# Expert rows spread over their half of the partitions, and every other pair of experts with its halves exchanged

## The chip, the cores and the metric

The kernel runs on one core of one Trainium2 chip, as one program and one launch. The time is that of the device in microseconds (us), as the median over runs. "The profiled execution" is one run recorded by the hardware profiler; positions in it are us from the start of its span. The core has five engines with queues of their own: PE (TensorE, with PEld for its weight loads), DVE (VectorE), ACT (ScalarE), POOL (GpSimd) and SP (SyncE, which here only issues DMAs), and sixteen DMA engines that all of them share. Every DMA raises its semaphore by sixteen, one for each DMA engine, and a wait for it asks for all sixteen.

## What is computed

Two transformer blocks follow one another on 512 tokens of width 1024, in fp32. The first mixes a sliding-window attention, a forgetting attention and a recurrent unit and ends in a dense feed-forward layer. The second mixes an mLSTM and a differential attention and ends in a layer of experts. Only this last layer is touched by the change:

```python
def hierarchical_moe(h, ...):        # h: 512 x 1024
    g_idx = top group of 4           # from h @ w_rg + b_rg
    j_idx = top 2 of the 8 experts of that group      # from h @ w_re + b_re
    combine = one_hot(e_idx) * weights                # 512 x 32, two entries a row
    for e in range(32):
        act = silu(h @ w_gate[e]) * (h @ w_up[e])     # 1024 -> 256
        y = y + combine[:, e:e+1] * (act @ w_down[e]) # 256 -> 1024
```

A token takes two experts, both of one group, so 1024 rows are worked in all, 32 an expert on average. The reference's own router, evaluated on the inputs, gives these counts for experts 0 to 31:

```
39 70 43 25 39 44 50 74   35 40 48 23 34 23 28 19
32 18 11 17 13 16 15 18   16 27 16 44 45 47 14 41
```

Experts 0 to 15 get 650 rows and experts 16 to 31 get 374.

## The kernel before, in words

**Dense part.** Nearly all of the time goes to dense products over 2048-column slabs of weights (`SLABS`). SP loads a slab, ACT rounds it to a high part `WH` (L975), DVE takes the rest `WL` (`feed`, L1505), and PE makes three products of high and low parts (L2354 to L2356). A slab's products begin once its `WL` is there (`lo_ready`, L2362). Their sums lie in four banks of PSUM in turn, and DVE or ACT evicts them (L2045 for the last projection `wo2`). `begin(s)` on DVE puts small work ahead of a slab's split: at the slab `("wo2", 0)` it calls `routing_numbers` (L1936), which makes constant tables, and then `feed`, which splits the slab after it.

**The expert layer.** A *tile* is a pair of experts with 128 rows of tokens: partitions 0 to 63 (half 0) for the one, 64 to 127 (half 1) for the other; `CAP` = 64 rows an expert. Expert x below 16 stands in half 0 and x + 16 in half 1 of the same tile. Tiles 0 to 2 hold experts 0 to 2 with 16 to 18; tile 3 (`OVER`) holds the rows beyond 64 of experts that have more (here 6 rows of expert 1 and 10 of expert 7); tile t from 4 to 16 holds experts t - 1 and t + 15. Further tiles run under a branch that is not taken here.

*Routing on DVE.* `places[:, 0]` is 0 or 64 by expert (its half), `places[:, 1]` its tile. The rank of a token within its expert comes from products with a triangular matrix (`ranks`); `row` is rank plus half (up to L2250). `inrow` (L2252) compares `row` with `iota`, a table of 128 numbers along the free axis that is 0, 1, 2 ... 127, and so says for each token which of the 128 partitions it takes; `here` (L2256) does so for the tile, with the first numbers of `iota`. Two sets of small products turn these into `tok` (the token of each partition and tile, or a number out of bounds for an empty place) and `wtab` (the weight).

*POOL* gathers with an indirect DMA the rows of a tile from `h2_dram` into `Xg` (L911, two buffers), and after the tile adds its rows `Yt` to `out` with an indirect DMA that accumulates (L929). Each takes 128 partitions of 4 KB, and places out of bounds are left out. The order of issue is gather(t + 2), scatter(t). A scatter waits for the one before it to have landed. For tile 3 there are two scatters, one for each half, the second behind the first.

*SP* loads an expert's weights: gate and up, 1 MB each, then down, 1 MB, into one of six slots (`SLOTS`, three tiles). Each is a DMA of 128 partitions with 8 KB in each. Tiles 0 to 2 are loaded early, each half at a place of its own among the slabs. From tile 3 on `load_pair` issues gate and up of both experts, once tile t - 3 has used its slots (`gu_done`), and then both downs, once `y_done` of tile t - 3 is reached (L746, L756).

*PE*, for each tile: `gate_up` (L2902, 32 products with 512 columns), the transposes of the next tile's rows (L2880), two transposes of the activations (L2888), `down` (L2919, 16 products). ACT and DVE do silu, the product, the copies and the weighting between them. `gate_up(t)` waits for its weights with all sixteen of each DMA:

```python
for half in halves(t):
    pe.wait_ge(*when(f"gu_landed{(2 * t + half) % SLOTS}", 32 * loads_before(t, half)))
```

Of the kernel before, what the change touches and what calls it, by code (L numbers as in the profile page):

```python
# [21 lines left out]
ALU = mybir.AluOpType  # L22
# [21 lines left out]
NE = 32  # L44
# [7 lines left out]
CAP = P // 2  # L52
NOV = (2 * S - 1) // (CAP + 1)
BASE = NE // 2 + 1
NPAIR = BASE + NOV - 2
# [314 lines left out]
def build_program(nc, a, out):  # L370

    ctx = ExitStack()
    with ctx:
        sems, shared = {}, dict(SHARED)

        def S_(name):
            name = shared.get(name, (name, 0))[0]
            if name not in sems:
                sems[name] = ctx.enter_context(nc.semaphore(name))
            return sems[name]  # L380

        def when(name, value):

            return S_(name), shared.get(name, (name, 0))[1] + value
# [4 lines left out]
        def at(name, kb, shape, dt=F32):  # L389
            return nc.alloc_sbuf_tensor_at(name, [P] + list(shape), dt, offset=int(base + kb * KB))[:]  # L390
# [4 lines left out]
        ones = at("ones", 6.5, [P])  # L395
# [107 lines left out]
        iota = at("iota", 110.8125, [P])  # L503
# [28 lines left out]
        thr = at("thr", R0 + 11.5, [2, 7])  # L532
        places = at("places", R0 + 11.5625, [2, NE])
# [8 lines left out]
        def K(name, w=None):  # L542
            return cst[:, CO[name]:CO[name] + (w or CW[name])]
# [4 lines left out]
        here = K("onehot", 2 * NB * NPAIR).rearrange("p (n j) -> p n j", j=NPAIR)  # L548
# [122 lines left out]
        for n in range(0, N_PARTS, 2):  # L671
            u = parts[n]
            t = n + 2 if u["end"] else n + 3
# [34 lines left out]
        for rows, tile in ((ROWS_A, rowsA), (ROWS_B, rowsB)):  # L708
            r = 0
            for name, n in rows:  # L710
                v = a[name]
                if name in ("q_norm_w_2", "k_norm_w_2"):
                    vec_dmas += [(tile[r:r + 1, DH * j:DH * j + DH], v) for j in range(2)]
                else:
                    names = "abc"[:len(v.shape) - 1]
                    if names:
                        lhs = " ".join(names)
                        v = v.rearrange(f"{lhs} (r p) -> ({lhs} r) p", p=P)
                    else:
                        v = v.rearrange("(r p) -> r p", p=P)  # L720
# [16 lines left out]
        def load_gate_up(sp, t, half, e):  # L737

            n = (2 * t + half) % SLOTS
            gate_up = WE[n][:, 0:KC * 2 * DE].rearrange("p (g k n) -> p g k n", g=2, k=KC)  # L740
            one = e if isinstance(e, slice) else bass.ds(e, 1)
            if t >= SLOTS // 2:
                sp.wait_ge(*when("gu_done", t - SLOTS // 2 + 1))
            for g, w in enumerate((a["w_gate_2"], a["w_up_2"])):

                sp.dma_start(gate_up[:, g].unsqueeze(1), w[0].rearrange("e (p k) n -> p e k n", p=P)[:, one]  # L746
                             ).then_inc(S_(f"gu_landed{n}"), 16)

        def load_down(sp, t, half, e):

            n = (2 * t + half) % SLOTS
            down = WE[n][:, KC * 2 * DE:].rearrange("p (k n) -> p k n", k=2)
            one = e if isinstance(e, slice) else bass.ds(e, 1)
            if t >= SLOTS // 2:
                sp.wait_ge(*when("y_done", t - SLOTS // 2 + 1))
            sp.dma_start(down.unsqueeze(1), a["w_down_2"][0].rearrange("e (p k) n -> p e k n", p=P)[:, one]  # L756
                         ).then_inc(S_(f"down_landed{n}"), 16)

        def load_expert(sp, t, half, e):
            load_gate_up(sp, t, half, e)  # L760
            load_down(sp, t, half, e)

        def load_pair(sp, t, experts):

            for half, e in enumerate(experts):
                load_gate_up(sp, t, half, e)
            for half, e in enumerate(experts):
                load_down(sp, t, half, e)
# [8 lines left out]
        def y_stores(t):  # L777

            return 16 * (t // 2 + 1 + (t >= OVER and t % 2 == OVER % 2))
# [9 lines left out]
        @block.sync  # L789
        def _(sp):  # L790
            for t in range(NB):
                sp.dma_start(xin[:, t, :], a["x"][0, P * t:P * t + P, :]).then_inc(S_(f"x_landed{t}"), 16)
            sp.dma_start(xm[0:M, :], a["meta_tokens"]).then_inc(S_("meta_landed"), 16)

            sp.dma_start(cst, a["const"]).then_inc(S_("cst_landed"), 16)
            for dst, src in vec_dmas[:len(ROWS_A)]:
                sp.dma_start(dst, src).then_inc(S_("rows_landed"), 16)
            for s in SLABS:
                if s["kind"] == "A":
                    n = s["a"]  # L800
                    if n == 0:
                        sp.wait_ge(*when("n_ffn_summed", KC))
                    if n >= ARAW:
                        sp.wait_ge(*when("ada_summed", n - ARAW + 1))
                    for dst, src in slab_dmas(s, araw[:, n % ARAW, :]):
                        sp.dma_start(dst, src).then_inc(S_(f"ada_landed{n % ARAW}"), 16)
                    continue
                n = s["h"]
                if n >= RAW:
                    slab_consumed(sp, W_SLABS[n - RAW])  # L810
                for dst, src in slab_dmas(s, raw[:, n % RAW, :]):
                    sp.dma_start(dst, src).then_inc(S_(f"raw_landed{n % RAW}"), 16)
                if s["name"] == ("kf", 1):

                    sp.wait_ge(*when("stage_ready", 8))
                    sp.dma_start(skew.rearrange("(p n) -> p n", p=P), stage.rearrange("p h n -> p (h n)")
                                 ).then_inc(S_("skew_written"), 16)
                if s["name"] == ("branch2", 1, 0):
                    sp.wait_ge(*when("dn_summed", C1))
                    load_expert(sp, 0, 0, 0)  # L820
                if s["name"] == ("wo2", 2):
                    sp.wait_ge(*when("m2_lo", KC))
                    load_expert(sp, 0, 1, NE // 2)
                if s["name"] == ("wo2", 3):
                    load_expert(sp, 1, 0, 1)
                if s["name"] == ("qf", 0):
                    sp.wait_ge(*when("skew_written", 16))
                    lines = skew[P - 1:P - 1 + P * (8 * SKEW - 1)].rearrange("(p n) -> p n", p=P)
                    for h in range(8):
                        sp.dma_start(sbias[:, h, :], lines[:, SKEW * h:SKEW * h + BAND]).then_inc(S_("sbias_landed"), 16)  # L830
            sp.wait_ge(*when("dense_ready", len(GROUPS)))
            load_expert(sp, 1, 1, NE // 2 + 1)
            sp.wait_ge(*when("h2_stored", 16 * NB))
            load_expert(sp, 2, 0, 2)
            sp.wait_ge(*when("n_two_summed", KC))
            load_expert(sp, 2, 1, NE // 2 + 2)
            sp.wait_ge(*when("overflow_ready", 1))
            load_pair(sp, OVER, [sp.value_load(eover[0:1, x:x + 1], min_val=0, max_val=NE - 1) for x in range(2)])
            for t in range(OVER + 1, BASE):
                load_pair(sp, t, (t - 1, t - 1 + NE // 2))  # L840
            with sp.If(more_tiles(sp)):
                for t in range(BASE, NPAIR):
                    x = t - BASE + 2
                    load_expert(sp, t, 0, sp.value_load(eover[0:1, x:x + 1], min_val=0, max_val=NE - 1))
                for n in range(2):
                    sp.wait_ge(*when(f"y_stored{n}", y_stores(NPAIR - 1 - (NPAIR - 1 - n) % 2)))
            for n in range(2):
                sp.wait_ge(*when(f"y_stored{n}", y_stores(BASE - 1 - (BASE - 1 - n) % 2)))
# [640 lines left out]
        def _(dve):  # L1489
            V = nc.vector  # L1490
            chain = Count(S_("dve_chain"))

            def link(ins):
                chain(ins)
                dve.wait_ge(chain.sem, chain.n)
# [440 lines left out]
            def routing_numbers():  # L1936
                link(V.tensor_scalar(later, K("expert"), -1000.0, None, ALU.add))

                link(V.tensor_tensor_scan(iota, ones, ones, -1.0, ALU.mult, ALU.add))
                link(V.tensor_scalar(thr[:, 0, :], iota[:, 1:8], float(CAP), 0.5, ALU.mult, ALU.add))  # L1940
                link(V.tensor_scalar(thr[:, 1, :], thr[:, 0, :], -1.0, None, ALU.add))
                link(V.tensor_scalar(places[:, 0, :], K("expert"), NE // 2 - 0.5, float(CAP), ALU.is_ge, ALU.mult))
                link(V.scalar_tensor_tensor(places[:, 1, :], places[:, 0, :], -0.5 * NE / CAP, K("expert"), ALU.mult, ALU.add))

                link(V.scalar_tensor_tensor(places[:, 1, :], places[:, 1, :], OVER - 0.5, places[:, 1, :], ALU.is_ge, ALU.add))

# [273 lines left out]
            def full_blocks(dst, x, limits):  # L2220
# [32 lines left out]
                            ALU.is_equal).then_inc(S_("dve_chain"), 1)  # L2253
            chain.n += 1
            at_pair = [P, 2 * NB, NPAIR]
            link(V.tensor_tensor(here, iota[:, 0:NPAIR].unsqueeze(1).to_broadcast(at_pair),  # L2256
                                 pair.unsqueeze(2).to_broadcast(at_pair), ALU.is_equal))
            V.tensor_tensor(inpair, here.unsqueeze(2).to_broadcast([P, 2 * NB, 2, NPAIR]),
                            ids.unsqueeze(3).to_broadcast([P, 2 * NB, 2, NPAIR]), ALU.mult).then_inc(S_("spots_ready"), 1)
# [691 lines left out]
```

## Time and profile before

| what | us |
|---|---|
| median of 3 runs (1743.67 to 1748.61) | 1747.85 |
| the profiled execution | 1746.53 |
| its span | 1744.7 |
| PE busy | 1604.5 |
| DVE busy | 808.8 |
| ACT busy | 544.8 |
| POOL busy | 78.4 |

The span is what the profiler recorded from the first to the last instruction of the core; the 1.8 us around it belong to the execution's own time. The median of the runs shown is 1.3 us above the profiled execution. Positions are read against the span. The expert layer's first gate/up product begins at 1459.4 and the span ends at 1744.7. "PE busy" counts matmuls whose ends are modelled, so it says that PE has work and not how fast that goes. In the chain of waits, "issue" is time in which an engine waited for nothing that the profile shows; a wait of several semaphores can hide a DMA there.

### The profile page before, as it was taken

How to read it: one execution, taken by the hardware profiler on the slowest of the kernel's cores; microseconds unless marked ns; L12 is line 12 of the kernel's file. 1: busy time of each engine (PE TensorE's matmuls, PEld its weight loads, DVE VectorE, ACT ScalarE, POOL GpSimd, SP SyncE). 2: the span in 40 equal slices, each digit the busy share in tenths (PEclk: the TensorE clock that was granted, in tenths of full speed). 3: DMA queues.
4: the chain of work that ended last, by engine and by line, in shares of the span. 5: the costliest groups of instructions: out<-in, count | busy, mean ns of one | idle time of the engine just before them, and what ended most of it. 6: DMA issues, size and time to landing. Idle time of an engine off the chain costs nothing.

```text
span 1744.7 us, 20138 instructions
## 1 busy us (share of the span) xinstructions
PE 1604.5 (92%) x8255; PEld 1203.5 (69%) x8255; DVE 808.8 (46%) x1383; ACT 544.8 (31%) x883; POOL 78.4 (4%) x99
## 2 busy tenths in 40 slices
PE   3999999999999999999998999999999975887775
PEld 3997777777788788888885787796778862333232
DVE  4456343455363767665224863446553533212121
ACT  5234353444433422222113423331543321111010
POOL 4000000000000000000000000000000001121111
PEclk8999999999999999999999999999999987989898
DMA  4333311122323466554222232221213537999992
GB/s 134 109 98 97 108 63 64 58 73 73 73 97 97 145 217 195 190 190 150 97 97 70 73 121 65 81 73 49 72 49 145 217 144 305 400 412 384 395 399 90
DMA packets 146800, 260.44 MB, mean 149 GB/s; under 512 B 16424, under 2 KB 121044, under 8 KB 133392
## 3 DMA queue, kind: packets, MB, share of 16 engines
q1 hardware_dynamic: 138512, 241.44, 39.4%
q0 software_dynamic: 8192, 17.67, 3.6%
q8 instruction: 67, 1.10, 0.3%
q14 instruction: 29, 0.24, 0.0%
HBM read 253.79 MB, written 15.25 MB: 154 GB/s over the span
## 4 chain that ended last, share of the span: by engine, by line
PE 83%; DVE 7%; issue 5%; ACT 2%; DMA 2%; POOL 0%; SPq 0%; POOLq 0%; DVEq 0%; ACTq 0%
PE psum L2354 20%; PE psum L2355 19%; PE psum L2356 19%; PE psum L2902 7%; PE psum L2919 4%; PE psum L2652 1%; PE psum L2641 1%; PE psum L2624 1%; PE psum L2880 1%; DMA Xg<-h_rows,tok 1%; DVE cst L1929 1%; DVE WL L1505 1%; PE psum L2551 1%; ACT Sb L1064 1%; PE psum L2571 1%
## 5 line engine op out<-in xcount | busy, mean ns | idle before, releaser
L2354 PE MATMUL psum<-AH,WH 128*128 128x512 f32 (+1 forms) x1208 | 479.0, 397 | 14.0 <-DVE AL L1551 6.3
L2355 PE MATMUL psum<-AL,WH 128*128 128x512 f32 (+1 forms) x1208 | 462.7, 383 | 0.0
L2356 PE MATMUL psum<-AH,WL 128*128 128x512 f32 (+1 forms) x1208 | 459.9, 381 | 0.0
L1505 DVE TENSOR_TENSOR WL<-raw,WH 128x2048 fp32r<-128x2048 f32 (+1 forms) x100 | 226.6, 2267 | 180.4 <-ACT WH L975 180.0
L2354 PEld LDWEIGHTS psum<-AH,WH 128*128 128x128 f32 x1208 | 230.2, 191 | 69.8 <-issue 12.3
L2356 PEld LDWEIGHTS psum<-AH,WL 128*128 128x128 f32 x1208 | 230.3, 191 | 44.8
L2355 PEld LDWEIGHTS psum<-AL,WH 128*128 128x128 f32 x1208 | 230.6, 191 | 43.7 <-issue 3.1
L975 ACT ACTIVATE WH<-raw 128x2048 fp32r<-128x2048 f32 (+1 forms) x100 | 189.0, 1890 | 137.8 <-PE psum L2356 104.3
L2902 PE MATMUL psum<-WE,XT 128*64 128x512 f32 x544 | 130.6, 635 | 22.2 <-issue 20.3
L2902 PEld LDWEIGHTS psum<-WE,XT 128*64 128x64 f32 x544 | 47.7, 147 | 103.1 <-issue 103.1
L2919 PE MATMUL psum<-WE,AT 128*64 128x512 f32 x272 | 66.5, 633 | 28.3 <-issue 26.7
L1929 DVE SCALAR_TENSOR_TENSOR cst<-araw,pcol,cst 128x256 f32<-128x256 f32 x168 | 81.6, 486 | 6.0
L1474 ACT ACTIVATE sA<-psum 128x256 f32<-128x256 f32 x17 | 6.5, 383 | 215.2 <-PE psum L2902 215.2
L2318 DVE TENSOR_TENSOR sA<-sA,psum 128x256 f32<-128x256 f32 x17 | 7.2, 422 | 133.3 <-ACT sA L1474 133.3
L2354 PE MATMUL psum<-FH,WH 128*128 128x512 f32 x176 | 68.7, 390 | 0.0
L2356 PE MATMUL psum<-FH,WL 128*128 128x512 f32 x176 | 68.6, 390 | 0.0
L2355 PE MATMUL psum<-FLo,WH 128*128 128x512 f32 x176 | 68.6, 390 | 0.0
L2354 PE MATMUL psum<-OH,WH 128*128 128x512 f32 x160 | 66.2, 414 | 0.0
L2919 PEld LDWEIGHTS psum<-WE,AT 128*64 128x64 f32 x272 | 22.6, 144 | 60.6 <-issue 60.6
L2355 PE MATMUL psum<-OL,WH 128*128 128x512 f32 x160 | 63.1, 394 | 0.0
L2356 PE MATMUL psum<-OH,WL 128*128 128x512 f32 x160 | 62.8, 393 | 0.0
L2326 DVE SCALAR_TENSOR_TENSOR Yt<-psum,wtab,g2row 128x512 f32<-128x512 f32 x34 | 24.0, 746 | 79.1 <-PE psum L2919 79.1
(514 smaller groups left out, 2043.0 us busy)
## 6 DMA issues: line engine op xcount, KB each, us to landing
raw<-w_in SPq DMA_DIRECT2D x45, 1024.0 KB, 5.2
WE<-w_gate SPq DMA_DIRECT2D x34, 1024.0 KB, 15.5
WE<-w_up SPq DMA_DIRECT2D x34, 1024.0 KB, 30.7
WE<-w_down SPq DMA_DIRECT2D x34, 1024.0 KB, 28.5
araw<-w_ada SPq DMA_DIRECT2D x24, 1024.0 KB, 5.4
raw<-w_ffn_in SPq DMA_DIRECT2D x22, 1024.0 KB, 7.9
raw<-w_ffn_out SPq DMA_DIRECT2D x11, 1024.0 KB, 4.8
raw<-w_out SPq DMA_DIRECT2D x8, 1024.0 KB, 5.0
```

What stands on the lines that cost most here:

```text
L975: nc.scalar.activation(WH[:, fed[0] % HL, 0:w], raw[:, fed[0] % RAW, 0:w], ACT.Copy).then_inc(S_("hi_ready"), 1)
L1064: nc.scalar.activation(p, p, ACT.Exp, scale=-1.0, bias=peak, accum_out=stat[:, 20 + m % 4:21 + m % 4]).then_inc(S_("mix_exp"), 1)
L1505: V.tensor_tensor(WL[:, n, 0:w], raw[:, n, 0:w], WH[:, fed[0] % HL, 0:w].bitcast(F32), ALU.subtract).then_inc(S_("lo_ready"), 1)
L1929: ins = V.scalar_tensor_tensor(acc, w[:, c, :], col("c_2", c), acc, ALU.mult, ALU.add)
L2326: V.scalar_tensor_tensor(Yt[:, t % 2, 512 * n:512 * n + 512], bank(4 + n), wtab[:, t:t + 1], g2row[:, 512 * n:512 * n + 512], ALU.mult, AL ...
L2354: MM(dst, lh, rh, start=first, stop=False)
L2355: MM(dst, lh, rl, start=False, stop=False)
L2356: return MM(dst, ll, rh, start=False, stop=last)
L2551: MM(bank(2 + 2 * (n % 2) + m, P * (i + 1)), qkd[half, 0, h, P * i:P * i + P], qkd[half, 1, h, 0:P * (i + 1)], start=True, stop=False)
L2571: ins = MM(bank(7, P, P * i), vd[:, j, P * h:P * h + P], dPT[:, m % 2, P * j:P * j + P], start=j == 0, stop=j == i)
L2902: ins = MM(bank(3)[rows], XT[:, t % 2, P * k + CAP * half:P * k + CAP * half + CAP], WE[(2 * t + half) % SLOTS][:, 0:KC * 2 * DE].rearrang ...
L2919: ins = MM(bank(4 + n)[rows], AT[:, t % 2, P * j + CAP * half:P * j + CAP * half + CAP], WE[(2 * t + half) % SLOTS][:, o:o + 512], start=j ...
```

## The change

In `routing_numbers` the first 64 numbers of `iota` are written in another order. Position 8a + v (a and v from 0 to 7) gets the number 8 ((v - a) mod 8) + a instead of 8a + v. Rank r of an expert then lies in group r mod 8 of eight partitions of its half, at place (r // 8 + r mod 8) mod 8 in it. The other 64 numbers are these plus 64. It takes fifteen small writes from the constants `expert` (0 to 31), one for the copy plus 64, and the scan that made `iota` goes. `thr` and `here` read `expert` where they read `iota`.

In `places[:, 0]` the odd experts' half is exchanged: odd x below 16 goes to half 1 and x + 16 to half 0. SP loads the odd pairs in that order, and of tile 1 the half that is loaded first is now expert 17's. Tile 3's rows keep their halves. Nothing else changes: tiles, sizes, the number of DMAs, their queues and waits are as before.

```diff
                 if s["name"] == ("wo2", 3):
-                    load_expert(sp, 1, 0, 1)
+                    load_expert(sp, 1, 0, NE // 2 + 1)
...
             sp.wait_ge(*when("dense_ready", len(GROUPS)))
-            load_expert(sp, 1, 1, NE // 2 + 1)
+            load_expert(sp, 1, 1, 1)
...
             for t in range(OVER + 1, BASE):
-                load_pair(sp, t, (t - 1, t - 1 + NE // 2))
+                x = t - 1
+                load_pair(sp, t, (x + NE // 2, x) if x % 2 else (x, x + NE // 2))
...
             def routing_numbers():
                 link(V.tensor_scalar(later, K("expert"), -1000.0, None, ALU.add))
 
-                link(V.tensor_tensor_scan(iota, ones, ones, -1.0, ALU.mult, ALU.add))
-                link(V.tensor_scalar(thr[:, 0, :], iota[:, 1:8], float(CAP), 0.5, ALU.mult, ALU.add))
+
+                spread = iota[:, 0:CAP].rearrange("p (a v) -> p a v", a=8)
+                for a_ in range(8):
+                    link(V.tensor_scalar(spread[:, a_, a_:], K("expert")[:, 0:8 - a_], 8.0, float(a_), ALU.mult, ALU.add))
+                    if a_:
+                        link(V.tensor_scalar(spread[:, a_, 0:a_], K("expert")[:, 8 - a_:8], 8.0, float(a_), ALU.mult, ALU.add))
+                link(V.tensor_scalar(iota[:, CAP:], iota[:, 0:CAP], float(CAP), None, ALU.add))
+
+                link(V.tensor_scalar(thr[:, 0, :], K("expert")[:, 1:8], float(CAP), 0.5, ALU.mult, ALU.add))
...
+                odd = places[:, 0, :].rearrange("p (e j) -> p j e", j=2)[:, 1]
+                link(V.tensor_scalar(odd, odd, -1.0, float(CAP), ALU.mult, ALU.add))
...
-            link(V.tensor_tensor(here, iota[:, 0:NPAIR].unsqueeze(1).to_broadcast(at_pair),
+            link(V.tensor_tensor(here, K("expert", NPAIR).unsqueeze(1).to_broadcast(at_pair),
```

## Rows read from the trace of the kernel before

**Rows 1.** the page's slices of the whole span, 40 of 43.6 us each

```profile
PE   3999999999999999999998999999999975887775
DMA  4333311122323466554222232221213537999992
GB/s 134 109 98 97 108 63 64 58 73 73 73 97 97 145 217 195 190 190 150 97 97 70 73 121 65 81 73 49 72 49 145 217 144 305 400 412 384 395 399 90
```

**Rows 2.** the chain that ended last: start us, length us, what

```profile
1447.16 8.27 DMA Xg<-h_rows,tok
...
1519.27 8.48 DMA out<-Yt,tokover
...
1530.42 10.08 DMA Xg<-h_rows,tok
...
1564.65 6.87 PE psum L2902 x32
...
1578.34 6.87 PE psum L2902 x32
...
1592.04 4.73 issue
1596.76 9.30 PE psum L2902 x32
...
1651.28 9.35 PE psum L2902 x32
...
1669.25 7.09 PE psum L2902 x32
...
1719.21 7.10 PE psum L2902 x32
```

**Rows 3.** DMA from 1465 to 1596.8 us, its slices and its hardware queue

```profile
GB/s 0 99 423 423 425 329 382 422 428 377 361 417 420 408 372 425 421 420 413 423 412 408 417 395 393 426 428 420 359 409 425 425 372 394 426 388 371 367 402 395
DMA packets 8916, 50.81 MB, mean 385 GB/s; under 512 B 2280, under 2 KB 2280, under 8 KB 3157
...
q1 hardware_dynamic: 6463, 47.14, 86.7%
```

**Rows 4.** the hardware DMA queue from 1465 to 1651.3 us

```profile
q1 hardware_dynamic: 9181, 66.92, 87.1%
```

**Rows 5.** each engine, granted clock, DMA share and GB/s in two stretches

```profile
core 0: us, PE busy (x) PEld busy (x) DVE busy (x) ACT busy (x) POOL busy (x), PEclk, DMA share, GB/s
1500.00:1596.80 96.80, 78.61 (x366) 33.99 (x363) 20.59 (x44) 12.95 (x36) 19.43 (x15) 0.93 1.02 405
1596.80:1719.20 122.40, 94.53 (x406) 38.38 (x407) 21.27 (x48) 15.11 (x42) 15.24 (x12) 0.91 0.93 363
```

**Rows 6.** DMA packets from 1450 us to the end, and the software queue

```profile
DMA packets 17591, 99.84 MB, mean 338 GB/s; under 512 B 4392, under 2 KB 4392, under 8 KB 6440
...
q0 software_dynamic: 5040, 8.41, 11.7%
```

**Rows 7.** SP's DMA issues of tile 3's first loads

```profile
1469.29 0.36 SPq L746 DMA_DIRECT2D WE<-w_gate  x1
```

**Rows 8.** DVE in order of time, around `routing_numbers`

```profile
1366.15 0.42 DVE L1939 TENSOR_TENSOR_SCAN iota<-ones 128x128 f32<-128x128 f32 x1
1366.61 0.17 DVE L1940 TENSOR_SCALAR thr<-iota 128x7 f32<-128x7 f32 x1
1366.82 0.17 DVE L1941 TENSOR_SCALAR thr<-thr 128x7 f32<-128x7 f32 x1
...
1367.71 2.29 DVE L1505 TENSOR_TENSOR WL<-raw,WH 128x2048 fp32r<-128x2048 f32 x1
1369.92 0.74 DVE L2045 SCALAR_TENSOR_TENSOR hT<-psum,mod,hT 128x512 f32<-128x512 f32 x1
```

**Rows 9.** TensorE, first product of the slab that follows

```profile
1373.15 0.40 PE L2354 MATMUL psum<-AH,WH 128*128 128x512 f32 x1
```

**Rows 10.** DVE, the comparison that makes `here`

```profile
1442.52 0.40 DVE L2256 TENSOR_TENSOR cst<-iota,r 128x240 f32<-128x240 f32 x1
```

## The prediction

> **What bounds the kernel now.** I went from the page's slices to the stretch where they change. TensorE is at nine tenths in nearly every slice up to the 32nd; from the 35th to the 39th its digits fall, the DMA digits are 9 and the kernel moves 384 to 412 GB/s [rows 1]. That last part is the expert phase, and the chain that ended last says what paces it [rows 2]. Early on, a tile's first gate/up matmul follows the one before by 13.7 us (1564.65 to 1578.34): TensorE's own pace. From tile 9 on each begins only after idle time put down to "issue" (4.73 us before tile 9): at 1596.76 for tile 9, 1651.28 for tile 12, 1669.25 for tile 13 and 1719.21 for tile 16. Those eight starts are 17.5 us apart on average (122.45 / 7). `gate_up` waits there for expert weights alone (every other condition was met earlier), so the weights set the end.
>
> Are all sixteen DMA engines late? Tile 9's gate/up weights have just landed whole at 1596.8. In queue order that takes 6 x 6.29 + 4.19 = 41.9 MB since tile 3's first load (an expert is 3.146 MB, a pair 6.29 MB). But the hardware queue had moved 47.1 MB [rows 3]: 5.2 MB belonged to later tiles. At 1651.3 tile 12 needed 60.8 MB and 66.9 had been moved [rows 4]. A wait ends with the last engine, so some engines run far ahead of the one waited for: at 6.29 MB per 15 us the mean engine is 12.4 us, then 14.6 us, ahead of the slowest. And while this spread grew the core moved 405 GB/s; later, with the leaders held back by full buffers, 363 including the tail [rows 5].
>
> What loads engines unevenly? Weight loads have the same 128 rows of 8 KB each time. The other queue moves the token rows: 2048 packets of between 2 and 8 KB, that is 1024 rows of 4 KB gathered and 1024 added back, 8.4 MB [rows 6]. I take it that the place of a row among its tile's 128 partitions chooses its engine; today an expert's n rows fill the first n of its 64.
>
> **The price of a row.** Tile 3's loads are issued at 1469.29 [rows 7]; the slice from 1468.3 to 1471.6 moves 99 GB/s where the next moves 423 [rows 3], so the flow begins at 1470.8. From there to 1719.2 the slowest engine works 248.4 us, on 14 pairs less one pair's down weights (13.67 pairs). At full flow the slices show 420 to 428 GB/s [rows 3]; I take 420, so 15.0 us a pair and 205.0 us, leaving **43.4 us** for rows. At 425 it would leave 46.
>
> How many rows is that? The gathers of tiles 2 to 16 and the scatters of tiles 0 to 14 fall in this time. From the router's counts I placed every row under three readings of partition to engine, and give the row moves of the busiest engine, before and after:
> (a) each engine serves 8 neighbouring partitions: 240, then 136.
> (b) eight engines to a half, 4 neighbouring partitions each, over and over: 194, then 130 (mean 113).
> (c) partitions dealt out singly, 16 engines in turn: 135, then 129.
> The price of a move would be 0.181, 0.224 or 0.321 us. An 8 KB packet at full flow costs an engine 0.312 us; 4 KB by bytes 0.156, and an addition reads and writes, 0.312; their mean, 0.234 (an estimate from these rows), is nearest to (b). The pace decides too: under (a) the busiest engine has 8 rows in every tile and the excess should be constant, but from tile 9 to 13 it is 72.5 - 60 = 12.5 us in four tiles, from 13 to 16 50.0 - 45 = 5.0 in three [rows 2]. Under (b) it has 8, 4, 6, 4 gathered and 7, 8, 8, 4 added, 49 moves or 11.0 us, then 8 and 14, or 4.9. And (c) leaves no engine ahead, against the 5.2 MB. I take (b).
>
> The change's groups of eight partitions would suggest (a), and so 43.4 x 104 / 240 = 18.8 us to gain; by (b) it is 14.3, below. The Trainium skill (DMA: Bandwidth & Descriptors, The descriptor swizzle) gives for a 128-partition transfer engine = 8 x (partition >> 6) + ((partition >> 2) & 7), which is (b); by that rule, with which the falling excess agrees, the gain is the smaller one.
>
> **The change, part by part.**
> *Spreading ranks inside the half* and *swapping halves in odd pairs* go together: neither alters how many rows, tiles or bytes there are. The first gives each run of eight ranks one place per engine of its half; the second shares the low experts' 650 rows and the high experts' 374 between both sets of eight engines. Alone, the first leaves 145 moves, the second 186, both 130: 64 moves fewer on the busiest engine, x 0.224 = **-14.3 us** (-15.2 at 425 GB/s).
> *The first gather* is on the chain, 8.27 us, while weights still stream [rows 2]. Its busiest engine goes from 8 rows to 5. Bound below by 3 rows x 0.156 = 0.5 us, above by 3 x (0.156 + 0.312) with a weight packet between rows, 1.4. All later weights are released by this tile's matmuls, so it shifts the end. I take **-1.0**. The last scatter's busiest engine falls from 8 rows to 6: -0.5 at most, taken as **-0.2**.
> *Extra DVE work in `routing_numbers`.* Fifteen small writes of `iota`, one copy plus 64, one negation: 17 instructions at the 0.20 to 0.21 us from one start to the next there, 3.5 us, less the 0.46 of the scan: +3.0 [rows 8]. Behind it on DVE stands the weight split L1505 at 1367.71, done at 1370.0; it becomes 1373.0. TensorE's first product of that slab starts at 1373.15 [rows 9]: covered, with 0.1 us to spare. Taken as +0.1; with the cover gone +3.0. The eviction L2045 behind it comes as much later; its bank is wanted again only four chunks on.
> *`here` reads constants instead of `iota`:* same form and size, 0.40 us [rows 10], nothing. *Loads 1 and 17 swapped, and half the later pairs:* the same loads at the same places in SP's queue, POOL's queue untouched, nothing.
> *Next limit.* TensorE could run 13.7 us a tile. Tile 3 adds its rows in two scatters one after the other, 8.48 us, then gather 6 takes 10.08 [rows 2], which puts TensorE late; after the change it catches up with the weights only near tile 12, since 1592.0 + 3 x 13.7 = 1633.1 against weights due at about 1635 (1651.3 less the gain). This costs nothing at tile 16 unless TensorE is another 25 us late.
> Sum: -14.3 - 1.0 - 0.2 + 0.1 = **-15.4 us**. The profiled execution took 1746.53 us, 1.3 under the median of 1747.85; both shift alike, to 1731.1 and **1732.5**.
>
> **Rivals.**
> 1. *Reading (a)*: 240 to 136 moves, -18.8, and so 1728. Against it: the falling excess. 5%.
> 2. *A shared limit takes over.* With all engines evenly busy the flow might not pass the 405 GB/s of [rows 5]. Weights (88.1 MB) and rows by the end of loads (some 7.3 MB) at 405 take 235.5 us from 1470.8, to 1706.3, which still allows everything. At the 385 of the whole ramp [rows 3] it is 247.8 us, to 1718.6, against the 1724 at which the last down weights land now (1719.2 plus 5 for two loads): -5.5, with the small terms 1741. 9%.
> 3. *Rows already lie evenly (c)*: every half uses all sixteen engines, so 6 moves x 0.321 = -1.9, DVE +0.1: 1746. Against it: the bytes ahead. 5%. The Trainium skill (DMA: Bandwidth & Descriptors, Rules for kernel authors) says so of transfers to disjoint partition halves, that both spray across all 16 engines.
> 4. *Slower: the DVE delay uncovers.* If the 17 short instructions cost 0.5 us each, L1505 ends at 1378.0, TensorE stops 4.9 us, and then runs slowly as after the stop at 1592 (9.30 us for a gate/up that takes 7.09 at tile 13 [rows 2]), +2.2: in all +7.1. This decides from a delay of 3.15 us on; it ends slower only with (c) under it: 1753. 3%.
> 5. *The order of ranks does not reach the DMA engines*, because rows are assigned in the order of issue, not by partition: no gain, +0.1, 1748. 3%.
>
> **How the numbers follow.** The forecast has 75%, to 1732.5. A measurement here tells about 0.3%, 5.2 us, from no change. Faster by more: forecast, rivals 1 and 2, 0.89; same: rivals 3 and 5, 0.08; slower 0.03. The range runs from 1727 (reading (a), a gather gain of 1.4) to 1741 (shared limit; rival 4's delay on the forecast would be 1740), and leaves out rivals 3, 4 and 5.
>
> **What would show it.** Right: at tile 9's and 12's gate/up starts the bytes ahead of need fall from 5 and 6 MB to under 2; starts in the late tiles come about 16.6 us apart rather than 17.5; tile 16 begins near 1704; flow stays over 400 GB/s until then. Tile 0's gather lands in about 7 us. L1505 behind `routing_numbers` starts 3 us later and TensorE does not wait. Wrong: bytes ahead unchanged (row placement is not what spreads the engines); bytes ahead gone but late starts still 17.5 apart (a shared limit); or a hole in TensorE at 1373.

## The result, and the profile after

The changed kernel took 1730.01 us in the median of four runs (1728.48 to 1731.68), the kernel before 1748.23 (1743.67 to 1749.99). The ratio is 0.9903 with a 95% interval of 0.9886 to 0.992, which is a gain of 14.0 to 19.9 us. The profiled execution took 1731.44 us with a span of 1729.6; before it was 1746.53 and 1744.7. So the two profiles stand 15.1 us apart and the medians 18.2; the profiled execution of before lies 1.7 us under its median and that of after 1.4 over.

The first view is the page's slices of the changed kernel, 40 of 43.2 us each, for [rows 1].

```profile
PE   3999999999999999999999999999999994888785
DMA  4333321222232555565223132211113617999995
GB/s 136 110 99 91 106 73 50 73 74 74 61 94 97 164 182 187 190 196 179 92 97 93 60 112 85 86 49 64 59 50 146 225 54 301 397 414 402 405 409 189
```

The expert phase is still the part with a full DMA row, at 397 to 414 GB/s. It is as busy as before and shorter. Next the chain that ended last (start us, length us, what), for [rows 2]; L2913 is the line of gate/up products that was L2902.

```profile
1446.83 7.94 DMA Xg<-h_rows,tok
...
1458.70 9.93 PE psum L2913 x32
...
1518.79 7.86 DMA out<-Yt,tokover
...
1529.31 9.64 DMA Xg<-h_rows,tok
...
1575.54 6.87 PE psum L2913 x32
...
1589.23 6.87 PE psum L2913 x32
...
1603.06 7.09 PE psum L2913 x32
...
1616.98 2.05 issue
1619.03 7.09 PE psum L2913 x32
...
1632.94 3.29 issue
1636.23 9.91 PE psum L2913 x32
...
1704.10 8.42 PE psum L2913 x32
```

Tile 9 now starts at 1589.23, 13.69 us behind tile 8, without any wait, where it had waited 4.73 us for weights. The first wait for weights is 2.05 us before tile 11, and tile 16 starts at 1704.10. From there to the end of the span it is 25.5 us, as before. The gain is all there by tile 12: it starts at 1636.23 and not at 1651.28, 15.05 us earlier, and from tile 12 to 16 both kernels need the same, 67.87 and 67.93 us.

The hardware queue from 1464 us to tile 12's start shows where it came from, for [rows 4], and the engines' view of two stretches, for [rows 5]:

```profile
q1 hardware_dynamic: 8493, 61.90, 86.0%
```

```profile
core 0: us, PE busy (x) PEld busy (x) DVE busy (x) ACT busy (x) POOL busy (x), PEclk, DMA share, GB/s
1500.00:1589.20 89.20, 76.81 (x364) 33.49 (x362) 19.18 (x42) 12.95 (x36) 17.32 (x13) 0.96 1.02 408
1589.20:1704.10 114.90, 90.68 (x408) 37.20 (x404) 23.79 (x51) 15.11 (x42) 17.77 (x14) 0.94 1.02 405
```

Tile 12's gate/up weights need 60.8 MB to have landed. 61.9 had been moved, 1.1 MB ahead instead of 6.1, or 2.6 us of the whole core's flow instead of 14.6. The flow no longer falls in the second stretch: 405 GB/s where it was 363. Cut at 19.2 us before tile 16 starts, each kernel's second stretch shows where that comes from, first before, then after:

```profile
1596.80:1700.00 103.20, 80.66 (x348) 32.64 (x348) 17.91 (x41) 12.95 (x36) 13.66 (x11) 0.91 1.01 394
1700.00:1719.20 19.20, 13.88 (x58) 5.75 (x59) 3.36 (x8) 2.16 (x6) 1.58 (x1) 0.91 0.52 196
```

```profile
1589.20:1684.90 95.70, 76.36 (x341) 31.46 (x339) 19.18 (x42) 12.95 (x36) 15.77 (x12) 0.93 1.02 405
1684.90:1704.10 19.20, 14.31 (x69) 5.74 (x65) 4.61 (x9) 2.16 (x6) 2.00 (x2) 0.98 1.01 404
```

Before, most of the fall stands in the last 19.2 us, when SP has issued its last load (at 1699.5 us): the DMA engines are busy 0.52 of the time and move 196 GB/s. The leading ones have finished, and tile 16 waits for the others. Afterwards they are all busy to the end. Ahead of that the flow was only 3% lower (394 to 405).

DVE around `routing_numbers` in order of time, for [rows 8] (first the routine's first instruction before and after), and the one wait of TensorE that is new there (engine, line, for whom: us in total, times, longest):

```profile
1365.95 0.17 DVE L1937 TENSOR_SCALAR later<-cst 128x32 f32<-128x32 f32 x1
```

```profile
1365.59 0.17 DVE L1938 TENSOR_SCALAR later<-cst 128x32 f32<-128x32 f32 x1
1365.80 0.38 DVE L1943 TENSOR_SCALAR iota<-cst 128x8 f32<-128x8 f32 x2
1366.21 0.16 DVE L1945 TENSOR_SCALAR iota<-cst 128x1 f32<-128x1 f32 x1
...
1370.13 0.19 DVE L1956 SCALAR_TENSOR_TENSOR places<-places 128x32 f32<-128x32 f32 x1
1370.36 2.29 DVE L1506 TENSOR_TENSOR WL<-raw,WH 128x2048 fp32r<-128x2048 f32 x1
```

```profile
PEld psum L2365 <- DVE WL L1506: 0.2, 1, 0.2
```

The split of the weights starts at 1370.36 and not at 1367.71. The routine itself began 0.36 us earlier in this execution, so from its first instruction to the split it takes 4.77 us where it took 1.76: 3.01 more. TensorE waits 0.2 us for the split.

### The profile page after: what moved, and what is told of

The parts are those of the page before. It is cut to its first block, busy times and chain, and to the rows that moved or that the text cites. A ratio compares the mean times of both kernels' runs of the same rounds, so it can differ in the third digit from the quotient of the medians.

```text
span 1729.6 us, 20154 instructions
## 1 busy us (share of the span) xinstructions
PE 1601.8 (93%) x8255; PEld 1202.2 (70%) x8255; DVE 811.2 (47%) x1399; ACT 544.8 (31%) x883; POOL 78.3 (5%) x99
## 4 chain that ended last, share of the span: by engine, by line
PE 84%; DVE 7%; issue 4%; ACT 2%; DMA 2%; POOL 0%; SPq 0%; POOLq 0%; DVEq 0%; ACTq 0%
PE psum L2365 20%; PE psum L2366 19%; PE psum L2367 19%; PE psum L2913 7%; PE psum L2930 3%; PE psum L2663 1%; PE psum L2652 1%; PE psum L2635 1%; PE psum L2891 1%; DMA Xg<-h_rows,tok 1%; DVE cst L1930 1%; DVE WL L1506 1%; PE psum L2562 1%; ACT Sb L1065 1%; PE psum L2582 1%
## 5 line engine op out<-in xcount | busy, mean ns | idle before, releaser
L1506 DVE TENSOR_TENSOR WL<-raw,WH 128x2048 fp32r<-128x2048 f32 (+1 forms) x100 | 226.6, 2266 | 179.4 <-ACT WH L976 178.9
L2366 PEld LDWEIGHTS psum<-AL,WH 128*128 128x128 f32 x1208 | 230.4, 191 | 43.6 <-issue 3.1
L2913 PE MATMUL psum<-WE,XT 128*64 128x512 f32 x544 | 130.1, 633 | 13.9 <-issue 11.9
L2913 PEld LDWEIGHTS psum<-WE,XT 128*64 128x64 f32 x544 | 47.4, 146 | 94.3 <-issue 94.3
L2365 PE MATMUL psum<-WH,AH 128*128 128x256 f32 (+1 forms) x208 | 59.5, 286 | 0.9 <-DVE vf L2080 0.9
```

What stands on the lines that cost most here:

```text
L1506: V.tensor_tensor(WL[:, n, 0:w], raw[:, n, 0:w], WH[:, fed[0] % HL, 0:w].bitcast(F32), ALU.subtract).then_inc(S_("lo_ready"), 1)
L2365: MM(dst, lh, rh, start=first, stop=False)
L2366: MM(dst, lh, rl, start=False, stop=False)
L2913: ins = MM(bank(3)[rows], XT[:, t % 2, P * k + CAP * half:P * k + CAP * half + CAP], WE[(2 * t + half) % SLOTS][:, 0:KC * 2 * DE].rearrang ...
```

## The experiments

The dense part ahead of the experts ends at a slightly different moment in each execution: tile 0's gate/up starts between 1457.05 and 1464.78 us in kernels that differ up to there only by the small DVE work, the rows of the first gather and the order of two loads. So beside the whole time I read a **stretch**, from the start of tile 0's gate/up to that of tile 16, out of each kernel's chain of waits. It is 1719.21 - 1459.36 = 259.85 us before (tile 0's row is in the chain: `1459.36 9.74 PE psum L2902 x32`) and 1704.10 - 1458.70 = 245.40 after: **-14.45**. Each stretch comes from one execution.

### Each half of the change alone

`spread_only` undoes the exchange of halves; `halves_only` writes `iota` in the old order 0 to 127.

```diff
 spread_only, against the changed kernel
-                odd = places[:, 0, :].rearrange("p (e j) -> p j e", j=2)[:, 1]
-                link(V.tensor_scalar(odd, odd, -1.0, float(CAP), ALU.mult, ALU.add))
-                load_pair(sp, t, (x + NE // 2, x) if x % 2 else (x, x + NE // 2))
+                load_pair(sp, t, (x, x + NE // 2))
 halves_only, against the changed kernel
-                    link(V.tensor_scalar(spread[:, a_, a_:], K("expert")[:, 0:8 - a_], 8.0, float(a_), ALU.mult, ALU.add))
-                    if a_:
-                        link(V.tensor_scalar(spread[:, a_, 0:a_], K("expert")[:, 8 - a_:8], 8.0, float(a_), ALU.mult, ALU.add))
+                    link(V.tensor_scalar(spread[:, a_, :], K("expert")[:, 0:8], 8.0 * a_, None, ALU.add))
```

In `spread_only` the loads of experts 1 and 17 stand as before too.

> Ranks spread inside each half as in the change, halves not exchanged. By reading (b) the busiest DMA engine has 145 row moves (before 194, after 130): 49 x 0.224 = 11.0 us less than before, plus about 0.5 from the first gather, so near 1736 us, and tile 16's gate/up starts near 1708 (before 1719.2, after 1704.1). By (a) 240 to 148 moves: -16.6, near 1731, and within 2 us of the whole change. If the spread were worth nothing: 1748.

> Only the halves of odd pairs exchanged, ranks in their old order. By (b) 194 to 186 moves: -1.8 us, near 1746.5, tile 16 near 1717.5. By (a) 240 to 240: 1748. If the halves were what mattered (the low experts' 650 rows against 374): most of the 18 us, near 1732.

The chain of waits of `spread_only`, then of `halves_only`:

```profile
1462.65 9.67 PE psum L2911 x32
...
1712.20 7.10 PE psum L2911 x32
```

```profile
1460.79 9.44 PE psum L2911 x32
...
1717.76 7.10 PE psum L2911 x32
```

`spread_only` took 1735.12 us, ratio 0.993 (0.9907 to 0.9952); its stretch is 249.55, -10.3 against the forecast -11.0. `halves_only` took 1744.78 us, ratio 0.9993 (0.998 to 1.0007); its stretch is 256.97, -2.9 against -1.8; the whole time alone does not tell it from no change. Both are as reading (b) has it: the spread carries most, and the exchange, worth 2.9 alone, is worth 4.15 on top of the spread (249.55 to 245.40). Once ranks are spread, an engine's count follows the rows of its half, and the exchange evens the halves: 145 to 130 moves, where in the old order of ranks it is 194 to 186. (The counts listed ahead add up to 634 and 390 rows for the low and the high experts, not to the 650 and 374 given beside them and in the prediction; the counts of moves follow from the list itself and stand.)

The trace also has the times of the sixteen increments of a DMA's semaphore, one for each engine. For the last down weights of `spread_only` they come in two groups: eight within 5.3 us, and after a gap of 8.5 us the other eight within 3.3 us. For the load before it the gap is 10.4 us. By (b) one half's engines have 129 to 145 moves there and the other's 81 to 96. In the changed kernel all sixteen come within 5.9 us, and before the change within 20.2 us.

The Trainium skill (DMA: Bandwidth & Descriptors, Rules for kernel authors) says of two transfers to disjoint partition halves that both use all 16 engines. That is about separate transfers; for the halves of one 128-partition transfer these 4.15 us and the two groups of eight show otherwise.

### Which partitions share an engine

Two kernels keep the exchange and put ranks 0 to 31 and 32 to 63 elsewhere. `even_fours` is even over groups of four neighbouring partitions as (b) has them, and crowded by (a). `even_eights` is even over groups of eight, and crowded by (b).

```diff
 even_fours: in place of the fifteen writes
+                spread = iota[:, 0:CAP].rearrange("p (h a v) -> p h a v", h=2, a=8)
+                for h in range(2):
+                    for v in range(4):
+                        link(V.tensor_scalar(spread[:, h, :, v], K("expert")[:, 0:8], 8.0 * v + 32.0 * h, None, ALU.add))
 even_eights: in place of the fifteen writes
+                spread = iota[:, 0:CAP].rearrange("p (a w v) -> p a w v", a=8, w=2)
+                for w in range(2):
+                    for v in range(4):
+                        link(V.tensor_scalar(spread[:, :, w, v], K("expert")[:, 0:8], 8.0 * v + 32.0 * w, None, ALU.add))
```

> As the change, but eight ranks running go to eight groups of FOUR neighbouring partitions (0, 4, 8 ... 28), the second 32 ranks to partitions 32 on. By (b) 136 moves on the busiest engine, 6 more than the change: +1.3 us, near 1731.5, tile 16 near 1705.5. By (a) 208 moves, -5.8 us against before: near 1742. If placement does not choose the engine: as the change or as before, alike with even_eights.

> As the change, but within each group of EIGHT neighbouring partitions the first four are filled by ranks 0 to 31 and the last four by ranks 32 to 63; halves exchanged. Every group of eight is as evenly filled as in the change. By (a) 136 moves, as in the change give or take 1.3 us: near 1731. By (b) half of the engines have nearly all rows, 202 moves on the busiest: +1.8 us against before, near 1749.5, tile 16 near 1721. This run and even_fours tell (a) from (b).

The chain of waits of `even_fours`, then of `even_eights`:

```profile
1461.39 9.57 PE psum L2912 x32
...
1707.09 7.10 PE psum L2912 x32
```

```profile
1461.27 9.41 PE psum L2912 x32
...
1722.68 7.10 PE psum L2912 x32
```

`even_fours`: 1731.82 us, ratio 0.9911 (0.9877 to 0.9944), stretch 245.70. `even_eights`: 1748.6 us, ratio 0.9999 (0.9985 to 1.0013), stretch 261.41. They differ by 15.7 us in the stretch, with the same rows in the same halves and the same number of DVE writes of one size. This settles the mapping against (a), by which the second would have kept all of the gain and the first lost most of it. By (c) `even_eights` would have 238 moves on one engine against 135 before, 33 us more; it has 1.6. The sixteen increments of the last down weights of `even_eights` come in the groups that (b) counts: eight within 0.5 us, four between 14.6 and 17.2 us after the first, and the last four between 21.4 and 22.3 us. By (b) eight engines have 37 to 51 moves, four have 155 to 171 and four 193 to 202. Every even group of eight is no help if its first four partitions belong to one engine and its last four to another.

### The price of a row

`lump` is the kernel before (halves too) with eight ranks running put on one engine by (b); as in the change, `thr` and `here` read `expert`. The two below it are `lump` without the fetched rows and without the added rows, so their outputs lack them:

```diff
 lump: in place of the scan that made iota
+                spread = iota[:, 0:CAP].rearrange("p (h b k) -> p h b k", h=2, b=8)
+                for h in range(2):
+                    for k in range(4):
+                        link(V.tensor_scalar(spread[:, h, :, k], K("expert")[:, 0:8], 8.0, float(4 * h + k), ALU.mult, ALU.add))
+                link(V.tensor_scalar(iota[:, CAP:], iota[:, 0:CAP], float(CAP), None, ALU.add))
 lump_no_gather: in gather
-                                        in_offset=bass.IndirectOffsetOnAxis(ap=tok[:, t:t + 1], axis=0),
+                                        in_offset=bass.IndirectOffsetOnAxis(ap=nobody, axis=0),
 lump_no_scatter: in scatter
-                    rows = tokover[:, half:half + 1] if t == OVER else tok[:, t:t + 1]
+                    rows = nobody
```

`nobody` is a column of numbers out of bounds that DVE writes ahead of `tok`, one instruction more.

> The kernel before with ranks placed so that eight ranks running share one engine by reading (b): partitions 0 to 3 and 32 to 35, then 4 to 7 and 36 to 39, and so on; halves as before. By (b) the two busiest engines have 8 rows in every tile, 240 moves, 46 more than before: +10.3 us, near 1758.5, tile 16 near 1729.5. By (a) the busiest has 234 against 240: 1748 or a little less. By (c) 170 against 135: +11.

> The lump kernel with every gather's rows out of bounds, so that no row is fetched (Xg keeps what it had; all DMAs and waits are still issued). 120 fewer row moves on the busiest engine. If a gathered row costs its bytes, 0.156 us: -18.7 us against lump, near 1740, tile 16 near 1711. If both kinds cost the same 0.224: -26.9, tile 16 near 1702.5.

> The lump kernel with every scatter's rows out of bounds, so that nothing is added to the output. 120 fewer row moves on the busiest engine. If an added row costs its read and its write, 0.30 us: -36 us against lump, near 1722, tile 16 near 1693.5. If both kinds cost 0.224: -26.9, tile 16 near 1702.5. The two losses together should be 120 x 0.45 = 54 us as long as DMA paces both.

Their chains of waits, in that order:

```profile
1444.57 8.55 DMA Xg<-h_rows,tok
...
1457.05 9.54 PE psum L2910 x32
...
1728.57 7.10 PE psum L2910 x32
```

```profile
1451.00 7.37 DMA Xg<-h_rows,nobody
...
1462.31 9.85 PE psum L2912 x32
...
1715.86 8.80 PE psum L2912 x32
```

```profile
1458.87 9.28 PE psum L2912 x32
...
1675.87 2.35 issue
1678.23 8.78 PE psum L2912 x32
...
1693.84 6.88 PE psum L2912 x32
```

`lump` took 1756.89 us, ratio 1.0065 (1.0049 to 1.0082), with a stretch of 271.52: +11.7 against before, +10.3 forecast. Without gathered rows it is 253.55, -18.0 for 120 rows on the busiest engine, or **0.150 us** each; without added rows 234.97, -36.55 for 120, or **0.305 us** each. The two losses make 54.5 us, and 54 was forecast. In the last kernel tile 16 follows without a wait for weights, so 0.305 may be a little low. The whole times were 1742.53 us, ratio 0.9971 (0.9956 to 0.9986), and 1722.55, ratio 0.9868 (0.9844 to 0.9893). An added row costs twice a gathered one of the same 4 KB. A read and a write by bytes would come to that, but no run here shows the two apart.

### The DVE work alone

`same_work` issues the added instructions with their sizes, and writes the old order:

```diff
 same_work, against the changed kernel, halves as before
+                    link(V.tensor_scalar(spread[:, a_, a_:], K("expert")[:, a_:8], 1.0, 8.0 * a_, ALU.mult, ALU.add))
+                    if a_:
+                        link(V.tensor_scalar(spread[:, a_, 0:a_], K("expert")[:, 0:a_], 1.0, 8.0 * a_, ALU.mult, ALU.add))
+                link(V.tensor_scalar(odd, odd, 1.0, 0.0, ALU.mult, ALU.add))
```

> The change's 17 added DVE instructions in routing_numbers with the same sizes, but writing the old order 0 to 127, and halves as before: only the DVE work of the change. Forecast: L1505 behind it 2.6 to 3.0 us later, TensorE waits 0.2 us at most, 1748 as before. Rival: the delay stops TensorE, +2 to +7 us.

It took 1747.92 us, ratio 1.0011 (1.0001 to 1.0022), and its stretch (1464.78 to 1724.30) is 259.52, that of before within 0.3. Its view of waits has the same line as the changed kernel's, 0.2 us of TensorE behind L1506. The interval of the ratio just leaves 1 out on the slow side, and its middle is 1.9 us; the trace has only the 0.2. Its execution is 5.1 us longer than that of before, and `routing_numbers` already begins 5.35 us later there (1371.30 against 1365.95); from that point to tile 0's gate/up it takes 93.48 us where before took 93.41. So in this execution the added work cost next to nothing. Whether the 1.9 us of the whole time are real these runs can't tell. In any case rival 4's 5 to 7 us did not come.

### Behind the DMA engines

> The changed kernel with the rows of all gathers and of all scatters out of bounds: no row is fetched and none is added to the output; all DMAs and waits are issued as before. It asks what stands behind the DMA engines. Weights alone need 13.67 pairs x 15.0 = 205 us from their start, which would let tile 16 start 217 us after tile 0; TensorE's own pace with the stop at tile 3 gives 1589.2 + 7 x 13.7 = 1685.1, 226.4 us after tile 0 (the changed kernel 245.4). So TensorE paces it: 226 to 229 us, and 1711 to 1714 us in all. If rows cost nothing beyond what the change already removed: 245 us and 1730. First gather: 7.4 us as in lump_no_gather.

The edits are the two of `lump_no_gather` and `lump_no_scatter`, made in the changed kernel. The chain of waits, and the engines' view of a stretch in the middle:

```profile
1449.47 7.28 DMA Xg<-h_rows,nobody
...
1460.68 9.93 PE psum L2915 x32
...
1670.14 6.87 PE psum L2915 x32
...
1683.92 6.88 PE psum L2915 x32
```

```profile
1530.00:1660.00 130.00, 113.20 (x550) 49.91 (x548) 30.19 (x65) 19.43 (x54) 26.90 (x21) 1.00 1.02 416
```

It took 1708.28 us, ratio 0.9795 (0.9766 to 0.9823), with a stretch of 223.24. From 1587.98 to 1670.14 its tiles start 13.69 us apart, TensorE's own pace at a full granted clock. I expected 226 to 229 because I kept the changed kernel's stop at tile 3. Without rows it is 3.2 us shorter from tile 0 to tile 9 (127.30 against 130.53). Gather 6 lands in 8.68 us instead of 9.64, and most of the rest is TensorE at a lower clock behind the stop. The rows are of the `down` products after it, in the changed kernel and then without rows:

```profile
1542.70:1548.15 5.45, 5.45 (x18) 1.97 (x20) 0.00 (x0) 0.00 (x0) 0.00 (x0) 0.66 1.02 408
```

```profile
1543.24:1546.90 3.66, 3.65 (x18) 1.58 (x20) 0.00 (x0) 0.00 (x0) 0.00 (x0) 1.00 1.03 410
```

The granted clock is 0.66 there in the changed kernel, where TensorE had waited 2.04 us for gather 6, and 1.00 without rows, where it had waited 1.05 us. All rows together thus still cost the changed kernel 22 us, and below 223 us TensorE would decide. The 416 GB/s with all sixteen engines evenly on weights lies under the 420 I had assumed, by 1%, and shows no shared limit at 405.

## Why the prediction was right, point by point

**The slowest engine and the bytes ahead** were right. The surplus at tile 12 fell from 6.1 to 1.1 MB, and the stretch became 14.45 us shorter. The sixteen increments of a load show the slowest engine directly: 20.2 us between the first and the last before, 5.9 after.

**Reading (b)** was right, and the two `even` kernels show it apart from (a) and (c). What stood for it beforehand, the excess that falls from 12.5 us in four tiles to 5.0 in three, was a real trace of it: late tiles have few rows beyond rank 32. The Trainium skill (DMA: Bandwidth & Descriptors, The descriptor swizzle) states this mapping for a 1 MiB transfer to 128 partitions; these runs agree with it for indirect ones, by the 15.7 us between the two kernels.

**Moves times price** was the term that counted. Across the kernels that move all rows:

| kernel | moves on the busiest engine, by (b) | stretch us |
|---|---|---|
| changed | 130 | 245.40 |
| even_fours | 136 | 245.70 |
| spread_only | 145 | 249.55 |
| halves_only | 186 | 256.97 |
| before | 194 | 259.85 |
| same_work | 194 | 259.52 |
| even_eights | 202 | 261.41 |
| lump | 240 | 271.52 |

A least-squares line through the eight has 0.234 us a move, and none is more than 1.1 us off it. I had taken 0.224; the mean of 0.156 and 0.312, which I used only to choose a reading, was nearer. The weight flow that I had set 1% too high does not explain it: with 416 GB/s the same sum gives 41.7 / 194 = 0.215, still lower. What does explain it stays open. So -14.3 was forecast for this term, the stretch gave -14.45 and the line gives 64 x 0.234 = 15.0.

**The first gather** was mis-sized. I took -1.0 us for three rows fewer, on a weight packet standing between two rows. It fell by 0.33, from 8.27 to 7.94; with no row at all it still takes 7.37 or 7.28, so 8 rows cost about 0.9 us of it and the rest is there anyway. The 0.33 lies under my lower bound of 0.5 too, which was 3 rows by bytes: the term was 0.67 too large, and both bounds missed. The last scatter's -0.2 did not show either: from tile 16's start to the end it is 25.5 us in both kernels.

**The DVE work** came as computed: +3.01 for +3.0, and 0.2 us of waiting for 0.1. The cover was used up to within that.

**The late pace** was wrong as a sign to look for. I wrote that late tiles would start 16.6 us apart and not 17.5. As an average from tile 9 to 16 they do: 114.87 / 7 = 16.4. But from tile 12 on they start 17.0 apart in both kernels. I had spread an average over tiles that differ: in the half of the slowest engine the old order put 7 or 8 rows on it in the fuller tiles, and 4 in most late ones. By count it has 30 moves from tile 12's start to tile 16's before, and the busiest of the changed kernel has 36. The gain comes from full tiles, early, and the late ones have little to give. TensorE's own pace ruled through tile 10 and the weights from tile 11 on, where I had said near tile 12.

**Rivals.** Reading (a) and even rows (c) fell with the two `even` kernels, and assignment by order of issue (rival 5) with them, since only the places of the rows differ between the two. The shared limit did not come: the changed kernel holds 405 to 408 GB/s to its last weights, and 416 without rows. The slow rival did not come either. The measured 1730.0 lies 2.5 us under the 1732.5 forecast; the profiled executions, 15.1 apart where 15.4 was said, agree more closely than the medians. Part of that closeness is luck: the gather and the scatter were taken 0.9 us too large together, and the term of the moves a little too small. Why the medians stand 18.2 apart is open; their interval of 14.0 to 19.9 us holds all these figures.

What is left: the busiest engine has 130 moves against a mean of 112, 4 us at 0.234. A further evening, such as filling every other tile from the other end, would lower it to about 125 by count, some 1 us, at the cost of instructions on the routing chain. This was not tried.

## What to carry to other kernels

A wait for a DMA is a wait for the slowest of its engines, so compare the bytes that the queue has moved with the bytes that the waited-for transfer needs: if far more has been moved, the engines are uneven and the missing time is in their spread. Then look at what rides with the even transfers and fills its partitions from the bottom up, and count rows per engine from the data, tile by tile: the busiest engine's count times one price came within 1.1 us of every stretch in which all rows moved. Check a layout against the real mapping of partitions to engines, since one that looks even in groups of eight gained nothing when it was uneven in groups of four.

## What the runs showed that I had not expected

The rows behind one engine were not only worth an average: all of the gain lay in the tiles up to 12, though every tile's rows were moved to other partitions. And a gather whose 128 places are all out of bounds, so that it moves no row, still took 7.4 us from issue to landing while weights were streaming, nearly as long as one with 8 rows on its busiest engine.
